# Delta-rule trips of a two-block kernel: block-inverse levels and convolution passes placed anew, output norm with tokens on the partitions, first HGRN head prepared inside the last mLSTM trip

## What is computed

```python
def gated_delta_rule(q, k, v, g, beta):          # per head, chunks of tokens
    decay = jnp.exp(jnp.where(incl, gc[..., :, None] - gc[..., None, :], -jnp.inf))
    kk = jnp.einsum("bhncd,bhnjd->bhncj", k, k)
    m = jnp.where(strict, beta[..., :, None] * kk * decay, 0.0) + jnp.eye(C, dtype=f32)
    sol = lax.linalg.triangular_solve(m, rhs, left_side=True, lower=True, unit_diagonal=True)
...
    o = gated_delta_rule(...)
    o = rms_norm(o.astype(p.dtype), out_g)       # over the 128 values of a head
# the inputs q, k, v are silu(causal_depthwise_conv(x W, w)), four taps
...
    f_b = lb + (1.0 - lb) * jax.nn.sigmoid(hg_f)     # HGRN2: per head of 128
    logf_b = jnp.log(f_b)                            # then cumulative sums over a chunk
    k_b = (1.0 - lb) * jax.nn.sigmoid(-hg_f)
```

## Time and profile before

| | |
|---|---|
| median of three runs | 3257.05 us (3255.30 to 3257.16) |
| the profiled execution | 3257.62 us, its span 3255.8 us |
| mean granted TensorE clock | 0.987 |
| TensorE matmuls (PE) busy | 3099.9 us, 95% |
| VectorE (DVE) busy | 1552.4 us, 48% |
| ScalarE (ACT) busy | 873.4 us, 27% |
| GpSimd (POOL) busy | 1690.1 us, 52% |

### The profile page before, as it was taken

One profiled execution on the slowest core, in us unless ns is written; L12 is line 12 of the kernel. 1 busy time (PEld: TensorE's weight loads), 2 busy tenths in 40 slices (PEclk: granted clock), 3 DMA queues, 4 the chain that ended last, 5 costly groups with the idle time before them and its releaser, 6 DMA issues.

```text
span 3255.8 us, 43392 instructions
## 1 busy us (share of the span) xinstructions
PE 3099.9 (95%) x15168; PEld 2541.4 (78%) x15168; DVE 1552.4 (48%) x2121; ACT 873.4 (27%) x1447; POOL 1690.1 (52%) x1748
## 2 busy tenths in 40 slices
PE   8999989999999999999899999999989999999996
PEld 7877778878778778787788877778778887778685
DVE  6731245555655556655513134244455656531723
ACT  5421133332433333333201011011113333310411
POOL 0255544444444444444267776566645555456773
PEclk9999999999999999999999999999999999999998
DMA  6322222212222222222242233222232222323222
GB/s 243 133 75 91 94 74 78 77 58 72 76 79 76 75 73 71 77 90 78 97 178 93 90 106 127 90 97 103 92 117 79 84 78 77 111 72 123 78 103 77
DMA packets 53527, 306.47 MB, mean 94 GB/s; under 512 B 5044, under 2 KB 7220, under 8 KB 21716
## 3 DMA queue, kind: packets, MB, share of 16 engines
q1 hardware_dynamic: 34528, 248.53, 21.8%
q10 hardware_dynamic: 18932, 57.00, 4.6%
HBM read 284.74 MB, written 20.77 MB: 94 GB/s over the span
## 4 chain that ended last, share of the span: by engine, by line
PE 84%; DVE 10%; ACT 3%; issue 2%; DMA 1%; ACTq 0%; DVEq 0%
PE gemm_ps L428 21%; PE gemm_ps L430 21%; PE gemm_ps L429 21%; DVE arena L865 6%; PE bankC L564 2%; PE bankA L552 2%; PE gemm_ps L782 2%; ACT arena L1591 2%; DVE a_lo L865 2%; PE gemm_ps L784 2%; PE gemm_ps L783 2%; PE bankA L738 2%; DVE arena L871 1%; ACT a_hi L1591 1%; PE bankB L585 1%
## 5 line engine op out<-in xcount | busy, mean ns | idle before, releaser
L428 PE MATMUL gemm_ps<-a_hi,w_hi 128*128 128x512 f32 (+1 forms) x3472 | 1379.9, 397 | 20.5 <-DVE a_lo L865 13.8
L430 PE MATMUL gemm_ps<-a_hi,w_lo 128*128 128x512 f32 (+1 forms) x3472 | 1333.0, 384 | 0.0
L429 PE MATMUL gemm_ps<-a_lo,w_hi 128*128 128x512 f32 (+1 forms) x3472 | 1330.6, 383 | 0.0
L404 POOL CAST w_hi<-w_raw 128x512 fp32r<-128x512 f32 x872 | 537.4, 658 | 1518.9 <-issue 1354.9
L396 POOL TENSOR_TENSOR w_lo<-w_raw,w_hi 128x512 fp32r<-128x512 f32 x872 | 1156.7, 1357 | 4.3
L428 PEld LDWEIGHTS gemm_ps<-a_hi,w_hi 128*128 128x128 f32 x3472 | 657.3, 189 | 154.8 <-issue 20.2
L430 PEld LDWEIGHTS gemm_ps<-a_hi,w_lo 128*128 128x128 f32 x3472 | 656.0, 189 | 130.5
L429 PEld LDWEIGHTS gemm_ps<-a_lo,w_hi 128*128 128x128 f32 x3472 | 657.7, 189 | 125.4 <-issue 9.0
L865 DVE TENSOR_TENSOR arena<-gemm_ps,arena 128x512 f32<-128x512 f32 (+3 forms) x161 | 107.0, 665 | 611.5 <-PE gemm_ps L430 492.3
L1591 ACT ACTIVATE arena<-arena 128x512 f32<-128x512 f32 (+6 forms) x398 | 224.6, 564 | 453.6 <-DVE arena L865 368.6
L865 DVE RECIPROCAL arena<-arena 128x512 f32<-128x512 f32 (+2 forms) x70 | 172.8, 2468 | 265.4 <-ACT arena L1591 263.3
(11 more groups left out here) (168 smaller groups left out, 2529.9 us busy)
## 6 DMA issues: line engine op xcount, KB each, us to landing
w_raw<-w_stream SPq DMA_DIRECT2D x236, 1024.0 KB, 4.8
y_scratch<-arena ACTq DMA_DIRECT2D x20, 512.0 KB, 3.4
arena<-y_scratch ACTq DMA_DIRECT2D x13, 512.0 KB, 4.0
arena<-gc_scratch ACTq DMA_DIRECT2D x12, 512.0 KB, 3.7
arena<-x_t ACTq DMA_DIRECT2D x2, 2048.0 KB, 9.9
arena<-y_scratch ACTq DMA_DIRECT2D x1, 4096.0 KB, 25.3
x_scratch<-arena ACTq DMA_DIRECT2D x1, 4096.0 KB, 14.4
y_out<-arena ACTq DMA_DIRECT2D x4, 1024.0 KB, 3.9
```

Source lines behind the costliest of these rows:

```text
L404: pool.tensor_copy(part(w_hi, w, q), part(w_raw, w, q)).then_inc(pool_step, 1)
L428: pe.matmul(o, hi, a_hi[:, k, 0:width], start=(k == 0), stop=False)
L429: pe.matmul(o, hi, a_lo[:, k, 0:width], start=False, stop=False)
L430: last = pe.matmul(o, lo, a_hi[:, k, 0:width], start=False, stop=(k == KT - 1))
```

## The change

1. `DN_STEPS` gets other weights. `values` goes from 13 to 8, so the first `half` comes after 20 k-steps in place of 25. Each `half` gets a weight of 1 (before 0), so one k-step stands between it and its `whole`, and a level takes five k-steps in place of four. `head_out` (24) becomes `head_out` (9) and `head_turn` (14). The sum stays 96.
2. VectorE's three taps of tile 1 (k) are spread: one at the tile's end, one after the `whole` of level 4, one after that of level 5. Taps of a tile that ends inside the recurrence are held until after the next `output`. ScalarE's silu of tile 1 is held until the levels are done.
3. The outputs of the recurrence have tokens on the partitions: the operands of the output matmuls are swapped, and they go to `bankC` for chunks 0 and 2 and `bankB` for 1 and 3. ScalarE squares each chunk with a running sum (`accum_out`). Four matmuls with a single moving column (128x1) replace the two 128x512 sums of the q term, and the two others go. The root and the reciprocal are taken on 128x2 and 128x8. VectorE scales the output, TensorE turns it back by eight transposes (`head_turn`), and VectorE multiplies it with gain and gate in one instruction per head. TensorE waits in `rest` of chunks 2 and 3 for ScalarE's reads (`o_read`) and in `head_turn` for `o_scaled`.
4. The last mLSTM mixing gets weights 30, 18, 14, and `hg_next` of the first HGRN2 head (38) behind them, in VectorE's and ScalarE's order between the ends of tiles 1 and 2.

```diff
-DN_STEPS = ([("natural", 12), ("values", 13)]
-            + [(s, l, w) for l in range(1, LEVELS - 2) for s, w in (("half", 0), ("whole", 4))]
-            + [("half", LEVELS - 2, 0), ("whole", LEVELS - 2, 2), ("turn", 2)]
-            + [("half", LEVELS - 1, 0), ("whole", LEVELS - 1, 1), ("flip", 2), ("solved", 4)]
+DN_STEPS = ([("natural", 12), ("values", 8)]
+            + [(s, l, w) for l in range(1, LEVELS - 2) for s, w in (("half", 1), ("whole", 4))]
+            + [("half", LEVELS - 2, 1), ("whole", LEVELS - 2, 2), ("turn", 2)]
+            + [("half", LEVELS - 1, 1), ("whole", LEVELS - 1, 1), ("flip", 2), ("solved", 4)]
             + [(s, n, g) for n in range(NB) for s, g in (("rest", 2), ("output", 3))]
-            + [("head_out", 24)])
+            + [("head_out", 9), ("head_turn", 14)])
+SPREAD_TAPS = {("whole", LEVELS - 3): (2,), ("whole", LEVELS - 2): (3,)}
 ML_STEPS = [("ml_scores", 30), ("ml_sums", 30), ("ml_out", 40)]
+ML_LAST = [("ml_scores", 30), ("ml_sums", 18), ("ml_out", 14), ("hg_next", 38)]
...
# TensorE
+                        if n >= 2:
+                            pe.wait_ge(s["o_read"], NB * j + n - 1)
                         for a in range(2):
-                            pe.matmul(bankC[:, a, b], St[:, a, :], qd[:, a, b], start=True, stop=False)
+                            pe.matmul(out_chunk(n, a), qd[:, a, b], St[:, a, :], start=True, stop=False)
...
-                        last = pe.matmul(bankC[:, a, n * P:n * P + P], u_[:, a, :], dT[:, a, n, :], start=(n == 0),
-                                         stop=True)
-                    if n == NB - 1:
-                        last.then_inc(s["o"], 1)
-                elif step[0] == "head_out":
+                        last = pe.matmul(out_chunk(n, a), dT[:, a, n, :], u_[:, a, :], start=(n == 0), stop=True)
+                    if n == 0:
+                        for i in range(NB):
+                            last = pe.matmul(out_bank(0)[:, 0, 2 * P + i:2 * P + i + 1], q_sq[:, i * P:i * P + P],
+                                             ones[:, 0:1], start=True, stop=True)
+                    last.then_inc(s["o"], 1)
+                elif step[0] == "head_turn":
+                    pe.wait_ge(s["o_scaled"], j + 1)
                     for a in range(2):
-                        pe.matmul(bankB[:, a, :], ones, q_sq, start=True, stop=False)
-                    for a in range(2):
-                        pe.wait_ge(s["o_sq"], 2 * j + a + 1)
-                        pe.matmul(bankB[:, a, :], ones, sqr[:, a, :], start=False, stop=True).then_inc(s["o_sum"], 1)
+                        for n in range(NB):
+                            last = pe.transpose(bankA[:, a, n * P:n * P + P], o_nat[:, a, n, :], ident)
+                    last.then_inc(s["o_turned"], 1)
...
# VectorE
+                    v.wait_ge(s["o_read"], NB * j + NB)
+                    op(v.reciprocal, o_rt, o_rt)
+                    for k in range(2):
+                        op(v.tensor_tensor, o_nat[:, :, k::2, :],
+                           out_bank(k)[:, :, 0:2 * P].rearrange("p a (n t) -> p a n t", n=2),
+                           o_rt[:, :, k::2, None].to_broadcast([P, 2, 2, P]), ALU.mult,
+                           sem=s["o_scaled"] if k else None, value=j + 1)
+                elif step[0] == "head_turn":
                     v.wait_ge(s["gate"], j + 1)
+                    v.wait_ge(s["o_turned"], j + 1)
                     for a in range(2):
-                        v.wait_ge(s["o_root"], 2 * j + a + 3)
-                        op(v.reciprocal, ort[:, a, :], ort[:, a, :])
-                        op(v.scalar_tensor_tensor, yo[:, a, :], bankC[:, a, :], gains(C_DNOUT), ort[:, a, :],
-                           ALU.mult, ALU.mult)
-                        op(v.tensor_tensor, yo[:, a, :], yo[:, a, :], z_g[:, a, :], ALU.mult,
-                           sem=s["dy_ready"], value=2 * j + a + 1)
+                        op(v.scalar_tensor_tensor, yo[:, a, :], bankA[:, a, :], gains(C_DNOUT), z_g[:, a, :],
+                           ALU.mult, ALU.mult, sem=s["dy_ready"], value=2 * j + a + 3)
...
# ScalarE
-                elif step[0] == "output" and step[1] == NB - 2:
-                    if g is not None:
+                elif step[0] == "rest" and step[1] == NB - 1:
+                    act.preload_act_table(ACT.Sqrt)
+                elif step[0] == "output":
+                    n = step[1]
+                    act.wait_ge(s["o"], NB * j + n + 1)
+                    if n == 0:
+                        op(o_eps, out_bank(0)[:, 0, 2 * P:2 * P + NB], ACT.Identity, bias=eps_q[:, :])
+                    for a in range(2):
+                        op(sqr[:, 0, a * P:a * P + P], out_chunk(n, a), ACT.Square,
+                           s["o_read"] if a and n < NB - 1 else None, NB * j + n + 1, accum_out=o_ss[:, a, n:n + 1])
+                    if n == NB - 2 and g is not None:
                         act.wait_ge(s["s_ready"], 3 * j + 3)
                         load_decay(g)
                 elif step[0] == "head_out":
-                    for a in range(2):
-                        op(sqr[:, a, :], bankC[:, a, :], ACT.Square, s["o_sq"], 2 * j + a + 1)
+                    for n in range(NB):
+                        op(o_rt[:, :, n], o_ss[:, :, n], ACT.Sqrt, s["o_read"] if n == NB - 1 else None, NB * j + NB,
+                           bias=o_eps[:, n:n + 1], scale=1.0 / P)
...
-                    for a in range(2):
-                        act.wait_ge(s["o_sum"], 2 * j + a + 1)
-                        op(ort[:, a, :], bankB[:, a, :], ACT.Sqrt, s["o_root"], 2 * j + a + 3, bias=eps_q[:, :],
-                           scale=1.0 / P)
```

87 lines of the change are left out of this document (56 added, 31 removed).

## The result

The changed kernel takes 3175.55 us (median of four runs, 3174.22 to 3176.4), the kernel before 3256.6 us beside it (3255.3 to 3257.16): a ratio of 0.9751, 95% interval 0.9734 to 0.9768. The forecast was 3175. The total agrees better than its terms do: the ten full looped trips won 62 us where 70 were forecast, and stretches that the forecast left alone made up for it.

A forecast was written before the change was run, and what follows sets the result against it. TensorE bounds the kernel, its matmuls busy 95% of the span. Ten looped trips at 7.0 us, plus 4.2 (first), minus 2.0 (last), plus 10.5 (HGRN2 head) give 82.7 us: 3257.6 to 3175 us, range 3160 to 3204 us.

The forecast's parts named there:

- Levels and taps: Inverse's levels and VectorE's taps in each looped trip: 5.6 us of waits lost, 5.0 us to be won.
- the residue: Loss left at the levels of a looped trip because VectorE's work fits with nothing to spare: 0.5 us.
- that just fits: Between a `whole` and the next `half`: VectorE's merge, transpose, merge, about 2.4 us and 0.2 latency, in 2.76 us.
- The norm: Recurrence outputs of each trip: four sums, 3.44 us, go; transposes and 128x1 matmuls come; net 2.0 us won.
- the single column: Four new 128x1 matmuls of the norm, eight records per trip: 0.6 us taken, at most 0.9 us.
- the rival of the slower kernel: Norm's chain ends late at `head_turn`, TensorE waits each trip; at 17 us the kernel takes 3266 us; chance 4%.
- The looped trip: One delta trip in the loop: 99.8 us less 5.0 for levels and taps and 2.0 for the norm, 92.8 us.
- levels stay bound by VectorE: Rival: each of six levels late by 0.35 us, a trip wins 2.1 us less, 3198 us; chance 18%.
- its own signs: Right: trip 92.5 to 93.5 us, no wait over 0.2 us at `half`; wrong: `half` waiting for VectorE's merges each trip.
- First and last trip: Delta trips at both ends, first `half` finds nothing ready: first trip wins 4.2 us, last 2 us longer.
- First HGRN2 head: Start of HGRN2: TensorE's 9.63 us wait for `hg_next` and the half clock behind it go, 10.5 us won.
- The margin: First HGRN2 head: VectorE done at 2402 to 2403, TensorE arrives at 2405.8.

The follow-up runs named there:

- the kernel with six k-steps: Changed kernel with a sixth k-step in levels 1 to 4 of every trip and `head_turn` four k-steps nearer the trip's end: 3173.78 us.
- the one with nothing between: Changed kernel with the k-step behind each `half` moved behind the `whole`, so nothing stands between the two: 3200.37 us.
- the one with the old last trip: Changed kernel with the old places of the levels in the delta trip behind the loop alone: 3177.05 us.
- the one with both edits: Changed kernel with levels of six k-steps in the loop and the old places of the levels in the trip behind it: 3176.38 us.

## Why the prediction was right, point by point

**Levels and taps: right in kind, 0.5 us too much.** Forecast 5.0 us per trip; the weights alone gave 2.56 and the taps 1.94, together 4.50. The taps are shown (1.94, most of it at a `half` and a chunk), and so is the k-step behind `half` (1.6 net). The mis-sized term is the residue. From the first `half` to `turn` it was to be 24.8 to 25.3 us, and it is 667.96 - 641.93 = 26.03: 1.26 us over the sum of the matmuls, for the 0.5 taken. The step that failed is "that just fits", VectorE's merge, transpose, merge between a `whole` and the next `half`. From the first record of `whole` at level 2 (649.28) the next `half` takes 3.73 us (653.01): 1.29 until the merge can start, 2.38 for the three instructions, 0.06 to TensorE. The room is 0.89 + 2.76 = 3.65 us, so the merge is 0.08 us late, and the first records behind such a late start come another 0.1 us slower. Level 3 has the same 0.2 us, level 4 has 0.3, level 5 has 0.1 (its slower first records alone) and level 1 has 0.4. There the three taps of tile 0, in a row still, end only at 645.01, ahead of the merge. That these are waits, and not what a change between dense and 128x128 work costs, is shown by the kernel with six k-steps, where 1.1 of the 1.26 us are gone.

**The norm: 1.73 us per trip for 2.0.** The 3.44 us went, the transposes cost 0.88 for the 0.85 taken. The mis-sized term is the single column: 0.6 us was taken, and the eight records cost 0.9, the upper end of the bound from the earlier trace rows. By the distances of starts, each with the dense matmul behind it, 3.44 - 0.88 - 0.90 = 1.66, within 0.1 of what was measured. The Trainium skill ("TensorE: Matmul & The Clock Gate", "Wait — 56ns, not 53.3ns?") says that with software decode a matmul of few columns is bound by a floor of about 62 ns. That floor is not what binds here: a record takes 0.112 us, as long as one of 128 columns. The chain to `o_scaled` was covered with 4.2 us to spare, so the rival of the slower kernel had nothing under it.

**The looped trip: 93.56 us for 92.8.** The two terms fall short by 0.8 us, 8 us in ten trips. The rival "levels stay bound by VectorE" named what happens: each `half` of levels 2 to 5 goes when VectorE's merge ends. It had it with 0.35 us late per level, where 0.1 to 0.4 were measured, 1.1 us per trip for 2.1; the range of the prediction held both. By its own signs the prediction is between right and wrong: no wait at `half` is over some 0.2 us and none is at `head_turn`, but `half` does wait for VectorE in each trip, and 93.56 us and 26.03 us lie outside 92.5 to 93.5 and 24.8 to 25.3.

**First and last trip.** First: 4.8 for 4.2, with the wait of 5.72 us in the range given. Last: the trip itself, taken from its `natural` to a later dense matmul, is 1.0 us longer (237.24 to 238.24) for the 2 forecast, with both waits as described. The stretch as a whole is 2.9 us shorter, which nobody forecast: behind the trip, a wait for VectorE, which has the scans of the gates (4x128) ahead of what TensorE needs, fell from 2.53 to 0.29 us, and 3.4 us at half the granted clock, which followed it before, aren't there any more:

```profile
1911.24 0.47 PE L440 MATMUL gemm_ps<-a_hi,w_hi 128*128 128x512 f32 x1 [0.29 <-DVE arena L881]
```

It is 0.29 in the changed kernel, the one with the norm alone, the one with taps in a row, the one with nothing between and the two with six k-steps behind the loop and the new places there; 2.5 us in all with the old norm, in the one with the old last trip and in the one with both edits, and 2.18 in the one with three times the single columns. The norm is thus not what decides. Nor is it the length of the scans: the eight of them take 4.13 + 2.92 = 7.05 us in the kernel before and in the one with the old last trip, where the wait is 2.5 us, and 2.54 + 5.48 = 8.02 in the changed kernel, where it is 0.29. Why the wait is short or long stays open. So the 3.9 us that lie there are luck.

**First HGRN2 head: 11.4 us for 10.5**, by the ledger, and 10.2 in these two stretches with that part alone. The direction and place were right. The margin was not: VectorE had 0.6 us to spare, not 3. It waits for ScalarE twice (1.56 and 0.65 us) and four scans took 4.89 us for 4.42.

**Sum.** Against the forecast's 82.7 us the ten looped trips gave 8 us too little. The last stretch gave 4.9 more than forecast, the last HGRN2 trip 2.3, the start 1.6, the HGRN2 head 0.9, the first trip 0.6 and the other HGRN2 trips 0.5, and the end took 2.1 away. The last HGRN2 trip is 81.3 to 81.8 us in every kernel but the one before, the one with the weights of the delta trips alone included, and the start moves between 426.4 and 429.7 us among kernels with the same code there. So the hit within 1 us is in part luck; the looped trips and the HGRN2 head carry 78 of the 83 us, where 85 were forecast for them.

## What to carry to other kernels

When one engine waits for a second in a chain of small steps, put a piece of its independent work between any two links, and see which long operations of the second engine stand ahead of a link: spreading three taps was worth 1.94 us per trip here, beside 2.56 for the new places and 1.73 for the norm. Price a small matmul by its records, not its columns: with a 128x128 float32 stationary block, one column costs what 128 do. Take the starts' distances as the measure of a chain, and compare the end of what it waits for with the start: here four waits of 0.1 to 0.2 us had no bracket at all. More room takes such a wait away, but look first at what moves next to the following step: here it cost more than it gave.

## What the runs showed of the hardware

The clock halved behind 24 single-column records (24 x 0.112 = 2.7 us of them) without any wait of TensorE, in four of twelve cases; behind eight such records it did in none.

How long a scan of VectorE takes depends on what GpSimd does beside it. Three scans of 4x128 in the kernel before, and GpSimd idle behind its last TENSOR_TENSOR (1974.81 + 1.74) until 1978.57:

```profile
1976.85 1.49 DVE L865 TENSOR_TENSOR_SCAN arena<-con,arena 4x128 f32<-4x128 f32 x3
```

```profile
1974.81 1.74 POOL L396 TENSOR_TENSOR w_lo<-w_raw,w_hi 128x512 fp32r<-128x512 f32 x1
1978.57 1.71 POOL L404 CAST w_hi<-w_raw 128x512 fp32r<-128x512 f32 x2 [2.02 <-issue]
```

The same scans in the changed kernel, in two groups of four, and GpSimd at the same time:

```profile
1899.94 2.54 DVE L881 TENSOR_TENSOR_SCAN arena<-con,arena 4x128 f32<-4x128 f32 x4
...
1903.46 5.48 DVE L881 TENSOR_TENSOR_SCAN arena<-con,arena 4x128 f32<-4x128 f32 x4
```

```profile
1900.23 2.66 POOL L416 CAST w_hi<-w_raw 128x512 fp32r<-128x512 f32 x4 [3.00 <-PE gemm_ps L442]
1902.94 5.73 POOL L408 TENSOR_TENSOR w_lo<-w_raw,w_hi 128x512 fp32r<-128x512 f32 x4
```

A scan takes 1.49 / 3 = 0.50 us with GpSimd idle, 0.64 beside the CAST and 1.37 beside TENSOR_TENSOR, about one scan for each of GpSimd's instructions (2.66 / 4 = 0.67 and 5.73 / 4 = 1.43 us). The Trainium skill ("SBUF — State Buffer", "Who interferes with whom") says that a VectorE instruction with two SBUF inputs contends with a GpSimd instruction that reads SBUF, and that the order of issue decides who is blocked. The trace agrees as far as durations can show it: the two take turns. A duration of VectorE taken from one place of a trace can be off by nearly a factor of three at another where GpSimd works; the scans of the HGRN2 head, 0.47 us longer than forecast, are of this kind, though no run isolates that.
